# Routing counts and key-list transposes each placed one step later in the TensorE program of a two-layer MoE backbone

## Chip, cores and metric

The kernel runs on one core of one Trainium2 chip. The metric is the device time of one execution in microseconds (us), the median of three runs. One further execution was taken by the hardware profiler; all rows below come from it.

## The reference

Two layers over 256 tokens of width 1024 (128 context tokens, 128 latent tokens). Each layer has a token-mixing part (three kinds of attention, merged and projected) and a mixture-of-experts part. Only the second matters here:

```
scores = sigmoid(x @ router_w);  biased = scores + router_bias
keep the 4 best of 8 groups of 8 experts, then the 6 best experts of a token
gates  = scores of those six, normalised, times 2.5
routed = sum over experts of gate * (silu(x @ w_gate) * (x @ w_up)) @ w_down   # 64 experts, hidden 256
shared = (silu(x @ shared_w_gate) * (x @ shared_w_up)) @ shared_w_down
y      = x + g2 * rms_norm(routed + shared)
```

Everything is float32. The experts' weights are 64 x 3 MB a layer and are used once.

## The kernel before

Every engine has its own program, written out by hand in the order in which it runs; semaphores join them. So an engine that waits holds up all that is written behind the wait, and nothing is reordered. "Layer" below is the Python loop `for l in range(DEPTH)`, with l = 0 first and l = 1 second.

**Weights.** SyncE (SP) loads every weight block into a ring of 12 slots of 1 MB in SBUF: 60 blocks a layer (one slot each), then 96 double blocks for the experts (two slots, 2 MB each). A load is issued when TensorE (PE) has freed its slots (`ring_free`, raised by `release` at a matmul); PE waits for a landing with `arrived` or `arrived_pair`. The next layer's first blocks follow the last experts' loads through the same ring.

**Routing.** PE forms the router's logits; VectorE (DVE) works out which six experts each token takes (`sel`, L1740, raises `sel_ready`), then the gate weights (L1743 to L1747) and the first half of the shared expert's hidden rows (`shared_hidden(0)`, L1699 and L1700). Meanwhile PE computes the shared expert: `shared_gate_up(t)` for token tile t is eight row steps k = 0 to 7, each one matmul of 128x128 by 128x512, which the trace shows as two instructions (float32 takes two passes). After some steps of `shared_gate_up(1)` PE waits for `sel_ready` and does the **routing counts**: column sums of `sel` (L989, L990), ranks of the tokens of experts 0 and 1 (L992 to L994, raises `ranks_done`), and two transposes of `sel` (L510, raises `keys_tr`). Then it finishes the steps.

DVE turns ranks and keys into `first_hot` (four instructions, L1758, `first_hot_ready`), which picks the tokens of the first expert pair; PE multiplies with it in `first_tokens` (L1002, L1005, `first_done`); DVE writes the first gather's row numbers (L1763, `first_rows`), does `shared_hidden(1)`, and enters the experts' loop.

**Key lists.** In that loop DVE extracts for each expert its up to 64 tokens: eight rounds of MAX8 and MATCH_REPLACE8 on `keys` (L1791/L1793 and L1796). The last MAX8 (L1793) raises `list_ready`. PE transposes the lists (`transpose_lists`, L1032, `list_tr`); DVE copies them (L1798) and writes the row numbers of all other pairs (L1799, `rows_ready`), and GpSimd (POOL) starts the indirect gathers of pairs 1, 2, ... (L498).

**Experts' loop.** 32 pairs of experts. For a pair g PE does `gate_up(g)` (L1050): eight row steps k, each two experts e side by side in two column halves, so four instructions a step; two experts together. Then `transpose_hidden(g)` (L510, waits for DVE's L1812), `down(g)` (L1076) and `combine(g)` (L1099). The order at the start is: transposes of pair 0's tokens, `gate_up(0)` with `transpose_lists` inside it, `transpose_inputs(1, 0)` (L510, waits for pair 1's gather), `transpose_hidden(0)`, `transpose_inputs(1, 1)`, `down(0)`, `gate_up(1)`. ScalarE (ACT) copies PSUM to SBUF (L1331) and does the tanh of the gates (L1338), DVE the products (L1804, L1812).

Of the kernel before, what the change touches and what calls it, by code (L numbers as in the profile page):

```python
# [32 lines left out]
KC = D // P  # L33
# [99 lines left out]
def hybrid_layers(nc, a, o):  # L133
    with ExitStack() as ctx:
# [191 lines left out]
        def wide(n):  # L326

            return ring[:, n % RING_SLOTS, :].rearrange("p (k n) -> p k n", k=4)
# [177 lines left out]
        def _(pe):  # L506
# [15 lines left out]
            for l in range(DEPTH):  # L522
# [3 lines left out]
                def arrived(n):  # L526

                    pe.wait_ge(ring_in[n % RING_SLOTS], (l * ROUNDS + n // RING_SLOTS + 1) * 16)

                def arrived_pair(n, base):  # L530

                    count = base + (n // RING_SLOTS + 1)
                    pe.wait_ge(pair_in[n % RING_SLOTS // 2], count * 16)
# [11 lines left out]
                def release(first, loads=1):  # L545
                    first.then_inc(ring_free, loads)
# [77 lines left out]
                for j in range(2):  # L624
# [3 lines left out]
                    for m in range(2):  # L628
                        for i in range(KC):
                            k = i % 2 * 4 + i // 2  # L630
# [305 lines left out]
                def token_rows(t, half):  # L936

                    for c in range(4):
                        last = transpose(PS[:, 4 + 2 * t + half, c * P:(c + 1) * P], h2T[:, 4 * half + c, t * P:(t + 1) * P])
                    last.then_inc(htok_tr, 1)  # L940

                def shared_gate_up(t, steps=range(KC)):
                    for k in steps:
                        if t == 0 and k % 4 == 0:
                            arrived(L_SH + k // 4)
                        last = pe.matmul(PS[:, 2 + t, :], h2T[:, k, t * P:(t + 1) * P], wide(L_SH + k // 4)[:, k % 4, :],  # L946
                                         start=(k == 0), stop=(k == KC - 1))
                        if t == 1 and k == 4:
                            release(last)
                    if k == KC - 1:  # L950
                        last.then_inc(shared_gu, 1)
# [31 lines left out]
                logits(1)  # L983
                for half in range(2):
                    token_rows(1, half)
                shared_gate_up(1, range(5))

                pe.wait_ge(sel_ready, l + 1)
                pe.matmul(PS[:, 0, 0:N_EXPERTS], ones, sel[:, 0, :], start=True, stop=False)  # L989
# [5 lines left out]
                for t in range(2):  # L995
                    last = transpose(PS[0:N_EXPERTS, 1, P + t * P:P + (t + 1) * P], sel[:, t, :])
                last.then_inc(keys_tr, 1)
                shared_gate_up(1, range(5, KC))

                def first_tokens():  # L1000
                    for t in range(2):
# [18 lines left out]
                with pe.Fori(0, npass) as p:  # L1020
# [6 lines left out]
                    def transpose_lists():  # L1027

                        pe.wait_ge(list_ready, q + 1)
                        apart(pe)  # L1030
                        for e in range(2):
                            last = pe.matmul(PS[e * CAP:(e + 1) * CAP, 2, 0:PAIRS], lists, ident[0:N_EXPERTS, e:N_EXPERTS:2],  # L1032
                                             start=True, stop=True)
                        last.then_inc(list_tr, 1)

                    def gate_up(g):

                        if g:
                            pe.wait_ge(xe_ready, done + (2 * g + 2))
                        for k in range(KC):  # L1040
                            if g == 0 and k % 4 == 0:
                                pe.wait_ge(xe_ready, done + (k // 4 + 1))
                            for e in range(2):
                                n = 6 * g + 2 * (k // 4) + e
                                if k % 4 == 0 and e == 0:
                                    arrived_pair(n, base)
                                if g == 0 and k == 2 and e == 0:
                                    transpose_lists()
                                w = ring[:, n % RING_SLOTS, :].rearrange("p (k c) -> p k c", k=4)
                                last = pe.matmul(PS[e * CAP:(e + 1) * CAP, 0, :], xe[:, k, e * CAP:(e + 1) * CAP], w[:, k % 4, :],  # L1050
                                                 start=(k == 0), stop=(k == KC - 1), skip_group_check=True)
                                if e == 0 and (k == 4 or (k == 0 and g >= 1)):
                                    release(last, 2)
                        last.then_inc(gu_done, 1)
# [54 lines left out]
                    for half in range(2):  # L1109
                        transpose_inputs(0, half)  # L1110
                    gate_up(0)
                    transpose_inputs(1, 0)
                    transpose_hidden(0)
                    transpose_inputs(1, 1)
                    down(0)
                    for g in range(1, PAIRS):
                        more = g + 1 < PAIRS
                        if not more:
                            pe.wait_ge(xe_ready, done + (2 * g + 2))
                            pe.wait_ge(first_hot_ready, uses * 4 + 8)  # L1120
                            first_tokens()
                        gate_up(g)
                        if more:
                            transpose_inputs(g + 1, 0, frees=2)
                        combine(g - 1, 0, frees=0 if more else 2)
                        transpose_hidden(g)
                        if more:
                            transpose_inputs(g + 1, 1)
                        combine(g - 1, 1)
                        down(g)  # L1130
# [804 lines left out]
```

## Time and profile before

| | us |
|---|---|
| three runs | 1704.34, 1704.36, 1705.16 (median 1704.36) |
| the profiled execution | 1704.68 |
| its span, first to last instruction | 1702.9 |
| PE busy in it | 1665.1 (98%) |
| DVE busy | 430.7 (25%) |
| ACT busy | 324.8 (19%) |
| POOL busy | 120.0 (7%) |

The mean granted clock of TensorE is 0.997 of its full speed. PE is busy nearly all the time, so the places where it is not, and what it waits for there, are read one by one from the order in time. The experts' loop of the first layer runs from about 371 to 859 us, that of the second from about 1207 to 1692 us; the change touches the stretch of some 20 us ahead of each and its first pair.

### The profile page before, as it was taken

The page shows a single profiled execution, that of the slowest core. Times are in us where ns is not written, and L with a number is a line of the kernel's source. Part 1 is how long each engine was busy: PE and PEld are TensorE (multiplying, and loading weights), DVE is VectorE, ACT ScalarE, POOL GpSimd, SP SyncE. Part 2 cuts the span into 40 slices and gives each one's busy share as a digit, 9 for nine tenths or more (in the row PEclk, how much of TensorE's full clock was granted, in tenths as well). Part 3 has the DMA queues.
Part 4 walks back from the last instruction along what each step waited for, and adds up shares of the span by engine and source line. Part 5 has one row for each costly group of instructions (what it writes and reads, how often), then busy time and mean ns, then how long its engine had stood idle before and what let it go on. Part 6 is the DMA issues. An engine that isn't in the chain of part 4 may idle for free. (4 is left out here: it accounts for less than half of the span.)

```text
span 1702.9 us, 21074 instructions
## 1 busy us (share of the span) xinstructions
PE 1665.1 (98%) x8107; PEld 892.7 (52%) x8107; DVE 430.7 (25%) x1183; ACT 324.8 (19%) x786; POOL 120.0 (7%) x164
## 2 busy tenths in 40 slices
PE   5999999999999999999999999999999999999998
PEld 3778788543333333333368878884433333333332
DVE  1114444361111111111131444543411111111112
ACT  1010341121111111111120113403111111111111
POOL 3001000020000000001020000001100000000000
PEclk9999999999999999999999999999999999999999
DMA  9994233379999999999999732235899999999993
GB/s 388 397 410 164 76 117 118 118 282 419 425 426 424 425 425 426 425 425 424 420 389 422 292 115 99 99 110 207 323 426 425 426 425 425 426 425 424 426 425 159
DMA packets 61100, 561.94 MB, mean 330 GB/s; under 512 B 13020, under 2 KB 13168, under 8 KB 21072
## 3 DMA queue, kind: packets, MB, share of 16 engines
q1 hardware_dynamic: 45504, 529.55, 75.4%
q0 software_dynamic: 15504, 31.09, 5.3%
q8 instruction: 66, 1.08, 0.3%
q14 instruction: 26, 0.21, 0.0%
HBM read 575.95 MB, written 6.88 MB: 342 GB/s over the span
## 5 line engine op out<-in xcount | busy, mean ns | idle before, releaser
L1050 PE MATMUL PS<-ring,region 128*64 128x512 f32 x2048 | 451.0, 592 | 0.7 <-ACT region L1331 0.7
L1050 PEld LDWEIGHTS PS<-ring,region 128*64 128x64 f32 x2048 | 146.4, 137 | 290.4 <-issue 290.3
L617 PE MATMUL PS<-region,ring 128*128 128x256 f32 x1088 | 245.3, 381 | 0.5 <-DMA ring<-in_blocks 0.5
L1099 PE MATMUL PS<-region 128*128 128x512 f32 x512 | 241.0, 594 | 0.0
L1076 PE MATMUL PS<-ring,region 128*64 128x512 f32 x1024 | 233.8, 598 | 0.2
L617 PEld LDWEIGHTS PS<-region,ring 128*128 128x128 f32 x1088 | 203.8, 190 | 34.2 <-issue 6.3
L1804 DVE SCALAR_TENSOR_TENSOR region<-region,PS 128x256 f32<-128x256 f32 x64 | 26.9, 421 | 662.8 <-ACT region L1338 662.8
L510 PEld LDWEIGHTS PS<-const,region 128*128 128x128 f32 (+1 forms) x925 | 106.5, 141 | 115.7 <-issue 67.3
L510 PE MATMUL PS<-const,region 128*128 128x128 f32 (+1 forms) x925 | 137.8, 278 | 15.7 <-DMA region<-in_c 9.6
L1076 PEld LDWEIGHTS PS<-ring,region 128*64 128x64 f32 x1024 | 67.7, 136 | 157.4 <-issue 156.7
L1344 ACT ACTIVATE region<-PS 128x512 f32<-128x512 f32 x128 | 76.4, 597 | 265.9 <-PE PS L1076 265.9
L1099 PEld LDWEIGHTS PS<-region 128*128 128x128 f32 x512 | 87.3, 190 | 65.6 <-issue 64.4
L498 POOL DMA_INDIRECT region<-h_table,region x62 | 61.3, 989 | 817.7 <-DVE region L1812 752.3
L1338 ACT ACTIVATE region<-PS 128x256 f32<-128x256 f32 x64 | 24.5, 384 | 406.0 <-PE PS L1050 406.0
L1331 ACT ACTIVATE region<-PS 128x512 f32<-128x512 f32 x128 | 76.2, 597 | 132.6 <-PE PS L510 132.6
L856 PE MATMUL PS<-region,ring 128*128 128x256 f32 x384 | 84.1, 380 | 0.0
L856 PEld LDWEIGHTS PS<-region,ring 128*128 128x128 f32 x384 | 72.6, 190 | 10.1 <-issue 0.3
L1812 DVE SCALAR_TENSOR_TENSOR region<-PS,region 64x256 f32<-64x256 f32 x128 | 61.9, 484 | 4.4
L904 PE MATMUL PS<-ring,region 128*128 128x512 f32 x128 | 55.6, 592 | 0.0
L560 PE MATMUL PS<-ring,condT 128*32 128x256 f32 x768 | 47.0, 394 | 6.7 <-DMA ring<-in_blocks 5.4
L1820 DVE TENSOR_SCALAR region<-const,region 128x256 f32<-128x256 f32 x64 | 22.6, 353 | 106.6 <-PE PS L1099 106.6
L1236 ACT ACTIVATE region<-PS,negm 128x128 f32<-128x128 f32 (+1 forms) x96 | 39.0, 415 | 34.8 <-issue 20.2
(270 smaller groups left out, 991.2 us busy)
## 6 DMA issues: line engine op xcount, KB each, us to landing
ring<-in_expert_blocks SPq DMA_DIRECT2D x192, 2048.0 KB, 17.1
ring<-in_blocks SPq DMA_DIRECT2D x120, 1024.0 KB, 19.6
region<-post_rows POOLq DMA_DIRECT2D x8, 512.0 KB, 6.2
h_first<-region POOLq DMA_DIRECT2D x4, 512.0 KB, 6.4
h_table<-region POOLq DMA_DIRECT2D x4, 512.0 KB
region<-in_w_kvk POOLq DMA_DIRECT2D x2, 640.0 KB, 18.6
region<-in_mla_w_ukv POOLq DMA_DIRECT2D x2, 512.0 KB, 21.8
region<-in_post_pack POOLq DMA_DIRECT2D x2, 512.0 KB, 25.4
```

The lines of the kernel that those rows point to most:

```text
L498: pool.indirect_dma_start(xg[:, g % XG, :] if g else xg[:, 0, 0:D], None, table if g else first_table, bass.IndirectOffsetOnAxis(ap=row_i[ ...
L510: return pe.transpose(out, in_, ident[0:n, 0:n])
L560: last = pe.matmul(PS[32 * g:32 * g + 32, MOD_BANK[group], half * 256:half * 256 + 256], condT[:, k, :], w[:, k % 2, 256 * g:256 * g + 256 ...
L617: last = pe.matmul(PS[:, j % 2, m * T:(m + 1) * T], w[:, k, m * P:(m + 1) * P], hT[:, k, :], start=(k == 0), stop=(k == KC - 1))
L856: last = pe.matmul(PS[:, b + n // 2, (n % 2) * T:(n % 2 + 1) * T], w[:, k, jj * P:(jj + 1) * P], src[:, k, :], start=(k == 0), stop=(k == 3))
L904: last = pe.matmul(PS[:, 4 + 2 * t + half, :], merged[:, k, t * P:(t + 1) * P], w[:, k % 4, :], start=(k == 0), stop=(k == KC - 1))
L1050: last = pe.matmul(PS[e * CAP:(e + 1) * CAP, 0, :], xe[:, k, e * CAP:(e + 1) * CAP], w[:, k % 4, :], start=(k == 0), stop=(k == KC - 1), s ...
L1076: last = pe.matmul(PS[e * CAP:(e + 1) * CAP, 2 + half, :], hid[:, f, e * CAP:(e + 1) * CAP], w[:, f, half * HALF:(half + 1) * HALF], start ...
L1099: last = pe.matmul(PS[:, 4 + 2 * t + half, :], hot[:, t * P:(t + 1) * P], og[:, half * HALF:(half + 1) * HALF], start=False, stop=True, sk ...
L1331: act.activation(xe[:, 4 * half:4 * half + 4, :].rearrange("p k s -> p (k s)"), bank(3 if g <= 1 and half else 1), ACT.Copy).then_inc(xe_r ...
L1344: act.activation(og[:, half * HALF:(half + 1) * HALF], bank(2 + half), ACT.Copy).then_inc(og_ready, 1)
L1812: ve.scalar_tensor_tensor(out=hid_rows[rows], in0=PS[rows, 0, 2 * P:4 * P], scalar=gate, in1=act_g[rows], op0=ALU.mult, op1=ALU.mult).then ...
```

## The change

Two steps of PE's program move; nothing is added or taken away, on PE or on any other engine.

```diff
-                shared_gate_up(1, range(5))
+                shared_gate_up(1, range(6))
 
                 pe.wait_ge(sel_ready, l + 1)
...
                 last.then_inc(keys_tr, 1)
-                shared_gate_up(1, range(5, KC))
+                shared_gate_up(1, range(6, KC))
...
-                                if g == 0 and k == 2 and e == 0:
+                                if g == 0 and k == 3 and e == 0:
                                     transpose_lists()
```

The first edit on PE, in both layers: one more row step (L946) of the shared gate/up stands ahead of the wait for `sel_ready` and the counts (L989 and on).

```order
 L934 MATMUL PS<-const,region 128x64 [waits parts_ready]
 L510 MATMUL PS<-const,region 128x128 x8
-L946 MATMUL PS<-ring,region 128x512 x5
+L946 MATMUL PS<-ring,region 128x512 x6
 L989 MATMUL PS<-sel,const 128x64 [waits sel_ready]
 L990 MATMUL PS<-sel,const 128x64
```

Six row steps instead of five come before the counts. Behind the counts and the two key transposes, still on PE, ahead of the wait for `shared_hid`:

```order
 L994 MATMUL PS<-sel,const 128x2
 L510 MATMUL PS<-const,sel 64x128 x2
-L946 MATMUL PS<-ring,region 128x512 x3
+L946 MATMUL PS<-ring,region 128x512 x2
 L510 MATMUL PS<-const,region 128x128 [waits shared_hid]
 L510 MATMUL PS<-const,region 128x128
```

Two steps are left there instead of three. The slot that step k = 4 frees is freed ahead of the counts in both kernels.

The second edit on PE, in `gate_up(0)` of each layer (L1050 a matmul of one expert, L1032 the list transposes, which wait for `list_ready`):

```order
 L533 ISA [waits xe_ready]
 L1050 MATMUL PS<-ring,region 64x512 [waits pair_in0]
-L1050 MATMUL PS<-ring,region 64x512 x3
+L1050 MATMUL PS<-ring,region 64x512 x5
 L1032 MATMUL PS<-const,region 64x32 [waits list_ready]
 L1032 MATMUL PS<-const,region 64x32
-L1050 MATMUL PS<-ring,region 64x512 x4
+L1050 MATMUL PS<-ring,region 64x512 x2
 L1042 REGISTER_ALU
```

The wait for `list_ready` now stands behind six matmuls (three row steps) instead of four, and two instead of four come before the wait for the second half of the weights.

## Rows read from the trace of the kernel before

**Rows 1.** The page: busy time of each engine.
```profile
PE 1665.1 (98%) x8107; PEld 892.7 (52%) x8107; DVE 430.7 (25%) x1183; ACT 324.8 (19%) x786; POOL 120.0 (7%) x164
```
**Rows 2.** Order in time, PE, first layer: start, us, line, shape, count, idle before.
```profile
352.18 4.46 PE L946 MATMUL PS<-ring,region 128*128 128x512 f32 x10
357.44 0.43 PE L989 MATMUL PS<-sel,const 128*128 128x64 f32 x2 [0.80 <-DVE sel L1740]
...
358.80 2.74 PE L946 MATMUL PS<-ring,region 128*128 128x512 f32 x6
361.38 0.38 PE L510 MATMUL PS<-const,region 128*128 128x128 f32 x2
361.60 0.51 PE L1002 MATMUL PS<-const,region 128*128 128x2 f32 x4
```
**Rows 3.** Order in time, DVE, first layer, routing and first tokens.
```profile
357.16 0.23 DVE L1740 TENSOR_SCALAR sel<-region 128x128 f32<-128x128 f32 x1
...
359.47 0.15 DVE L1751 TENSOR_SCALAR ranks<-PS 128x4 f32<-128x4 f32 x1
...
360.11 0.98 DVE L1758 TENSOR_SCALAR region<-const,ranks,sel 128x64 f32<-128x64 f32 x4
...
362.58 0.16 DVE L1763 TENSOR_SCALAR region<-PS 128x1 uint32<-128x1 f32 x1 [0.60 <-PE PS L1005]
```
**Rows 4.** Order in time, PE, first layer, the first pair.
```profile
370.96 1.94 PE L1050 MATMUL PS<-ring,region 128*64 128x512 f32 x8 [0.34 <-ACT region L1331]
373.32 0.30 PE L1032 MATMUL PS<-const,region 64*64 64x32 f32 x4 [0.43 <-DVE region L1793]
373.56 5.37 PE L1050 MATMUL PS<-ring,region 128*64 128x512 f32 x24
379.54 0.66 PE L510 MATMUL PS<-const,region 128*128 128x128 f32 x4 [0.61 <-DMA region<-h_table,region]
380.99 0.84 PE L510 MATMUL PS<-const,region 128*128 128x128 f32 x6 [0.79 <-DVE region L1812]
```
**Rows 5.** Order in time, DVE, first layer, end of the key lists.
```profile
372.76 0.42 DVE L1793 MAX8 region<-region 64x8 f32<-64x256 f32 x1
...
373.95 0.19 DVE L1798 COPY region<-PS 128x32 f32<-128x32 f32 x1
```
**Rows 6.** Order in time, PE, second layer, the same places.
```profile
1193.19 0.43 PE L989 MATMUL PS<-sel,const 128*128 128x64 f32 x2 [0.81 <-DVE sel L1740]
...
1206.71 1.94 PE L1050 MATMUL PS<-ring,region 128*64 128x512 f32 x8 [0.34 <-ACT region L1331]
1208.79 0.30 PE L1032 MATMUL PS<-const,region 64*64 64x32 f32 x4
...
1215.25 0.66 PE L510 MATMUL PS<-const,region 128*128 128x128 f32 x4 [0.85 <-DMA region<-h_table,region]
1216.56 0.84 PE L510 MATMUL PS<-const,region 128*128 128x128 f32 x6 [0.65 <-DVE region L1812]
```
**Rows 7.** Order in time, DVE, second layer.
```profile
1208.23 0.42 DVE L1793 MAX8 region<-region 64x8 f32<-64x256 f32 x1
...
1209.42 0.19 DVE L1798 COPY region<-PS 128x32 f32<-128x32 f32 x1
```
**Rows 8.** Order in time, POOL, first layer: pair 1's gather.
```profile
375.22 1.01 POOL L498 DMA_INDIRECT region<-h_table,region  x1 [9.95 <-DVE region L1799]
```
**Rows 9.** DMA issues at 376.5 us: KB, us to landing; the gather is pair 2's.
```profile
ring<-in_expert_blocks SPq DMA_DIRECT2D x1, 2048.0 KB, 8.5
region<-h_table,region POOLq DMA_INDIRECT x1, 8.7
```
**Rows 10.** Stretches: length, busy of PE, PEld, DVE, ACT, POOL, clock, DMA share, GB/s.
```profile
376.50:380.00 3.50, 2.89 (x16) 0.99 (x12) 0.57 (x2) 0.38 (x1) 0.99 (x1) 1.00 0.86 272
380.00:865.00 485.00, 484.07 (x2190) 186.07 (x2188) 76.78 (x183) 92.08 (x172) 31.77 (x35) 1.00 1.01 424
```
**Rows 11.** Order in time, PE, where the second layer begins.
```profile
865.75 1.07 PE L560 MATMUL PS<-ring,condT 128*32 128x256 f32 x16 [0.70 <-DMA ring<-in_blocks]
```

## The prediction

> **What bounds the kernel now.** The page first: PE is busy 1665.1 us of 1702.9, 98%, and beside its own weight loads (PEld) no engine is over 26% [rows 1]. So the time is PE's own work plus its idle pieces, and a change of order alone can win only idle pieces, or make new ones. The order in time of PE, DVE and POOL around the two edits then shows each idle piece and what ended it. The reader is to see four in each layer: PE waits for `sel` ahead of the counts (0.80 and 0.81 us idle) [rows 2, 6]; for the last MAX8 of the key lists (0.43 in the first layer, unmarked in the second) [rows 4, 6]; for pair 1's gather (0.61, 0.85); and for the hidden rows of pair 0, that is ACT's tanh and DVE's L1812 (0.79, 0.65) [rows 4, 6]. Last, the stretches by DMA share: from 380 to 865 us the 16 DMA engines are full (1.01) while PE is busy 484.07 of 485.00 us [rows 10], and 0.70 of the missing 0.93 is one wait for a weight block, where the second layer begins [rows 11]. In the first layer's experts' loop PE and the weight stream run nearly neck and neck.
>
> **First edit, one step more ahead of the counts.** A pass of a row step takes 0.43 us: six from 358.80 to 361.38 [rows 2]. Five steps are ten passes, 352.18 to 356.48; the counts start at 357.44, because `sel` is written at 357.16 + 0.23 = 357.39, 0.05 earlier [rows 2, 3]. (The 0.80 in the row counts from the modelled end of the last matmul; by starts it is 0.96.) A sixth step is 0.86 us and ends at 352.18 + 12 x 0.43 = 357.34. It fits into the wait with 0.1 us left: the counts start where they did. That is the cover of the moved work, and a thin one; were it gone, the counts would be late by what is missing, but DVE reads the ranks only at 359.47 [rows 3], when PE has long been at the next steps, from 358.80 [rows 2]. So up to half a us would be free.
>
> Behind the counts two steps are left, so PE comes to the transposes at 360.52 instead of 361.38, to `first_tokens` (L1002) at 360.74 instead of 361.60. There a new wait appears: `first_hot` is ready at 360.11 + 0.98 = 361.09 [rows 3], with the same 0.05 PE can start at 361.14. Of the 0.86 won, 0.46 stays. Out of an idle engine two short matmuls take 0.43 instead of 0.38 (L989 against L510) [rows 2], so I take 0.1 off: 0.36 us, bounds 0.30 and 0.46. Queued behind this new wait are only PE's own later steps.
>
> Who follows: DVE's L1763 waits for L1005 with 0.60 us idle [rows 3], so it comes 0.36 earlier, and with it everything in DVE's order: `shared_hidden(1)`, the eight rounds, the last MAX8. PE's shared down and pair 0's transposes run in one piece up to `gate_up(0)`, which starts at 370.60 instead of 370.96. SP's load that waits for the last shared down's release is 0.36 earlier too. In the second layer the same differences hold.
>
> **Second edit, the list transposes behind step k = 2.** First layer before: `gate_up(0)` starts at 370.96, steps 0 and 1 end at 370.96 + 4 x 0.43 = 372.68, the transposes start at 373.32: 0.64 idle by starts, since the MAX8 ends at 372.76 + 0.42 = 373.18 [rows 4, 5]. After: steps 0 to 2 end at 370.60 + 2.58 = 373.18; the lists are there at 372.82 plus the same 0.14, 372.96. No wait. The transposes cost 0.24 as before (373.32 to 373.56), then five steps of 0.86: `gate_up(0)` ends at 377.72, where it was 373.56 + 5.16 = 378.72. Gain 1.00 = 0.36 + 0.64. Second layer: the idle time there is 1208.79 - (1206.71 + 1.72) = 0.36 [rows 6], the MAX8 ends at 1208.65 [rows 7], 0.36 earlier in the new kernel, and PE is there at 1208.93: gain 0.36 + 0.36 = 0.72.
>
> The lists now wait for PE, not PE for the lists; is anybody late by that? DVE's copy L1798 comes after its own MATCH_REPLACE8, at 373.95, though PE's transposes end at 373.62 [rows 4, 5]. After: DVE is free for it at 373.59, the transposes end at 373.18 + 0.30 = 373.48: 0.36 earlier. In the second layer they end at 1208.93 + 0.30 = 1209.23, against a copy at 1209.42 [rows 7] that could have come at 1209.06: 0.15 to 0.19 earlier only. Pair 1's gather moves by as much: issued at 374.86 instead of 375.22 [rows 8], usable at 379.18 instead of 379.54; in the second layer at 1215.08 instead of 1215.25 [rows 4, 6]. It is the next wait in PE's order. Its four transposes take 0.44, and behind them PE waits for the hidden rows, which hang on the end of `gate_up(0)` and so come at 380.99 - 1.00 = 379.99 and 1216.56 - 0.72 = 1215.84. The gather's transposes are done at 379.62 and 1215.52. So the whole 1.00 and 0.72 reach `down(0)`, with 0.37 and 0.32 us to spare. Before, these margins were 1.01 and 0.87: they are what pays for the gain.
>
> **What is left of it at the end.** In the second layer nothing comes behind the experts' loop but PE's own work and the outputs, so 0.72 stays if the ring does not run dry. In the first layer PE's gain ends at the wait for a block [rows 11]: PE is there a full us earlier and waits longer, unless the stream is earlier as well. The stream begins with the load freed 0.36 earlier, and goes on with loads freed in `gate_up(0)`, a whole us earlier (the one issued at 376.5 [rows 9]). Between 376.5 and 380 the engines moved at a share of 0.86, later at 1.01 [rows 10]: 0.15 x 3.5 = 0.53 us of unused time, which the earlier loads fill. So the stream shifts by 0.36 + 0.53 = 0.89; its bounds are 0.36 (only its start moves) and 1.00 (every load was release-bound). I take 0.9.
>
> Sum against the profiled execution: 1704.68 - 0.9 - 0.72 = 1703.06. The median of the three runs is 0.32 below that execution, so the forecast is 1702.8, 0.1% under the 1704.36 of before.
>
> **A rule on the queues.** Pair 2's gather, issued at 376.5 while a weight load was starting, took 8.7 us [rows 9]; pair 1's, 1.3 us ahead of that, was usable after 379.54 - 375.22 = 4.3 us [rows 4, 8]. The Trainium skill (DMA: Bandwidth & Descriptors, "Queues, rings and completion order") says that each DMA engine takes turns between its queues, a packet at a time. It speaks against this change: the more weight packets stand in the other queue, the longer a gather takes. The pair of durations agrees in direction; by this rule the gather would be later than in my sum, which puts weight on the rival below.
>
> **Rivals.**
> - Slower: pair 1's gather meets the weight load. The load after it is issued a whole us earlier, the gather only 0.36 (second layer 0.72 and 0.17). So the lead shrinks from 1.3 to 0.7 us. If it takes the loaded duration, 8.7 us, it is usable at 374.86 + 8.7 = 383.56, 4.38 later than in my sum with 0.37 to spare: the first layer loses 4.0 - 1.0 = 3.0, of which the 0.70 at the layer's end can hide a part (2.3 left); the second 4.38 - 0.32 - 0.72 = 3.3. Sum +5.6: 1710.0. It decides from 0.37 us of delay on. Against: between 376.5 and 380 most of the gather's time already ran beside that load [rows 9, 10]. In full 3%. In a small form, a us late, it takes 0.6 and 0.7 of the gains: about 1704.0; 15%.
> - Stream-bound: the weight stream shifts by 0.36 only. Then the first layer gives 0.36: 1703.3. For it: the full DMA engines; against: the 0.86 share. 16%.
> - The edit does nothing because a neighbouring wait takes it all: with `first_hot` an idle start dearer than taken and the ring dry in the second loop, 1704.3. The order of PE shows both steps moved, so this is about time, not about the program. 5%.
> - More than forecast: later waits close as well, 1701.5. 4%.
> - The forecast, 1702.8, 57%; its own range is 1702.3 to 1703.3.
>
> **Numbers.** The range must hold the time 8 times in 10: 1701.8 to 1704.4, which takes in the small gather delay and the stream's bounds. About 0.2% (3.4 us) is what a measurement of this kernel can tell from no change. Only the full gather case lies above that; with something unseen, slower 4%, faster 3%, within 93%.
>
> **What would show it.** Counts still at 5.26 us after the start of the L946 row; a new PE idle of about 0.4 ahead of L1002, released by DVE L1758; no idle ahead of L1032 in either layer; `gate_up(0)` ending 1.0 and 0.7 earlier against the counts; a wait for the gather still there, and one for L1812 behind it; a wait for the block at the second layer's start of about 0.8 instead of 0.70; span 1701.3. I am wrong if the counts start later, if L1032 still waits, or if the gather's usable time after its issue grows beyond 4.7 us.

## The result and the profile after

The changed kernel takes 1718.45 us (median of 1716.91, 1718.13, 1719.13 and 1718.76), against 1704.63 us for the kernel before (four runs, 1704.34 to 1705.16): 1.0076 times as long, with a 95% interval of 1.0064 to 1.0089. The forecast was 1702.8 us in a range of 1701.8 to 1704.4, so the kernel became slower where it was to become faster, and the time lies outside the range. The profiled execution is the lowest of the four, 1716.91 us.

The page of the changed kernel, as in [rows 1], and its line for the short transposes:

```profile
span 1715.1 us, 21074 instructions
PE 1670.5 (97%) x8107; PEld 895.8 (52%) x8107; DVE 431.1 (25%) x1183; ACT 324.8 (19%) x786; POOL 120.3 (7%) x164
L510 PE MATMUL PS<-const,region 128*128 128x128 f32 (+1 forms) x925 | 140.4, 283 | 24.9 <-DMA region<-h_table,region 13.8
```

The span is 12.2 us longer, PE's busy time 5.4 us: some 7 us are new idle time, and 5 are work that took longer. The last row tells where to look: the transposes waited 13.8 us for data that came from `h_table`, a gather. In the kernel before, this line had 15.7 us of waits in all, 9.6 of them for the constants `in_c`, and 0.61 and 0.85 for this gather [rows 4, 6].

PE in order of time, first layer (start, busy us, what, then in brackets the idle time ahead and what ended it); answers to [rows 2, 4]:

```profile
352.01 5.32 PE L946 MATMUL PS<-ring,region 128*128 128x512 f32 x12
357.27 0.43 PE L989 MATMUL PS<-sel,const 128*128 128x64 f32 x2
...
360.98 0.61 PE L1002 MATMUL PS<-const,region 128*128 128x2 f32 x4 [0.25 <-DVE region L1758]
...
370.44 2.79 PE L1050 MATMUL PS<-ring,region 128*64 128x512 f32 x12 [0.34 <-ACT region L1331]
373.17 0.30 PE L1032 MATMUL PS<-const,region 64*64 64x32 f32 x4
373.40 4.51 PE L1050 MATMUL PS<-ring,region 128*64 128x512 f32 x20
384.67 2.40 PE L510 MATMUL PS<-const,region 128*128 128x128 f32 x10 [6.76 <-DMA region<-h_table,region]
387.00 4.01 PE L1076 MATMUL PS<-ring,region 128*64 128x512 f32 x16
390.84 7.03 PE L1050 MATMUL PS<-ring,region 128*64 128x512 f32 x32
```

The same in the second layer, answering to [rows 6]:

```profile
1214.88 4.51 PE L1050 MATMUL PS<-ring,region 128*64 128x512 f32 x20
1226.38 2.40 PE L510 MATMUL PS<-const,region 128*128 128x128 f32 x10 [7.00 <-DMA region<-h_table,region]
1228.71 4.69 PE L1076 MATMUL PS<-ring,region 128*64 128x512 f32 x16
1233.24 2.31 PE L1050 MATMUL PS<-ring,region 128*64 128x512 f32 x10
```

Everything up to the end of `gate_up(0)` is as forecast or nearly so. Then PE stands still for 6.76 and 7.00 us, where it waited 0.61 and 0.85 for the same gather [rows 4, 6]. And ten transposes then take 2.40 us. Who issued what, from POOL's and SP's rows (a start, the time in issue) and the view of DMA issues (KB, us from issue to landing), first layer; answers to [rows 8, 9]:

```profile
374.80 1.01 POOL L498 DMA_INDIRECT region<-h_table,region  x1 [9.69 <-DVE region L1799]
```

```profile
375.52 0.34 SPq L360 DMA_DIRECT2D ring<-in_expert_blocks  x1
```

```profile
ring<-in_expert_blocks SPq DMA_DIRECT2D x1, 2048.0 KB, 9.3
region<-h_table,region POOLq DMA_INDIRECT x1, 9.8
```

The weight load now follows the gather after 0.73 us (before 1.32; second layer 0.76, before 1.35; the times in the rows are rounded, so a difference of two can be off by 0.01), and the gather lands 0.16 us ahead of that whole 2 MB load, at 384.63 against 384.79. Below I call the time from POOL's issue of the gather to SP's issue of the next load the **lead**, and from POOL's issue to the start of PE's transposes the **gather time**.

The windows of the changed kernel (stretch and sum, then busy us of PE, PEld, DVE, ACT and POOL, the granted clock, the DMA share, GB/s):

```profile
378.00:380.00 2.00, 0.00 (x0) 0.00 (x0) 1.39 (x3) 0.34 (x1) 0.00 (x0) 1.00 0.98 407
380.00:382.00 2.00, 0.00 (x0) 0.00 (x0) 0.00 (x0) 0.00 (x0) 0.99 (x1) 0.73 1.00 422
382.00:384.00 2.00, 0.00 (x0) 0.00 (x0) 0.00 (x0) 0.00 (x0) 0.00 (x0) 0.50 0.65 259
384.00:386.00 2.00, 1.33 (x6) 1.33 (x7) 0.00 (x0) 0.18 (x1) 0.00 (x0) 0.50 0.26 98
386.00:388.00 2.00, 2.00 (x9) 1.10 (x10) 0.78 (x2) 1.02 (x2) 0.00 (x0) 0.56 0.65 131
388.00:390.00 2.00, 2.00 (x12) 0.58 (x10) 0.00 (x0) 0.60 (x1) 0.00 (x0) 1.00 0.79 311
```

While PE is idle, from 377.91 on, the granted clock falls to 0.50, that is 1.2 instead of 2.4 GHz, and it stays there while PE is at work again (from 384.67), for some 3 us. In the second layer it lasts longer, 4 to 5 us:

```profile
1228.00:1230.00 2.00, 2.00 (x8) 0.91 (x8) 0.74 (x2) 0.73 (x2) 0.00 (x0) 0.50 0.66 131
1230.00:1232.00 2.00, 2.00 (x10) 0.57 (x8) 0.00 (x0) 0.26 (x1) 0.00 (x0) 0.79 0.86 356
```

That is the work that took longer. In the first layer, from 382 us on, the DMA engines run empty as well: the next load needs slots that only PE's later steps free.

### The profile page after: what moved, and what is told of

It reads as the page before. It is cut to its first block and busy times, and to the rows that moved or that the text cites. A ratio compares the mean times of both kernels' runs of the same rounds, so it can differ in the third digit from the quotient of the medians.

```text
span 1715.1 us, 21074 instructions
## 1 busy us (share of the span) xinstructions
PE 1670.5 (97%) x8107; PEld 895.8 (52%) x8107; DVE 431.1 (25%) x1183; ACT 324.8 (19%) x786; POOL 120.3 (7%) x164
## 5 line engine op out<-in xcount | busy, mean ns | idle before, releaser
L1050 PE MATMUL PS<-ring,region 128*64 128x512 f32 x2048 | 450.9, 592 | 0.7 <-ACT region L1331 0.7
L1050 PEld LDWEIGHTS PS<-ring,region 128*64 128x64 f32 x2048 | 146.3, 137 | 290.5 <-issue 290.4
L510 PE MATMUL PS<-const,region 128*128 128x128 f32 (+1 forms) x925 | 140.4, 283 | 24.9 <-DMA region<-h_table,region 13.8
L856 PEld LDWEIGHTS PS<-region,ring 128*128 128x128 f32 x384 | 72.6, 190 | 10.1 <-issue 0.3
L1812 DVE SCALAR_TENSOR_TENSOR region<-PS,region 64x256 f32<-64x256 f32 x128 | 61.9, 484 | 4.4
```

Of the source, the lines that this page charges most:

```text
L510: return pe.transpose(out, in_, ident[0:n, 0:n])
L856: last = pe.matmul(PS[:, b + n // 2, (n % 2) * T:(n % 2 + 1) * T], w[:, k, jj * P:(jj + 1) * P], src[:, k, :], start=(k == 0), stop=(k == 3))
L1812: ve.scalar_tensor_tensor(out=hid_rows[rows], in0=PS[rows, 0, 2 * P:4 * P], scalar=gate, in1=act_g[rows], op0=ALU.mult, op1=ALU.mult).then ...
```

## Experiments

The theory from the two profiles (A): the load, issued 0.85 us earlier against the routing counts, takes the gather's bandwidth, and the clock adds to it. Rivals: (B) it is PE's own program, with another cause for the long gather, such as the fetch of instructions; (C) the whole loss is the wait, the clock costs nothing; (D) the gather is served only once the load is through. The expectations of e1, e2 and e4 call another rival C: that the first edit makes the gather late.

All gather times and leads, first / second layer, in order of the lead. The leads and gather times are those of the one profiled execution of each kernel. The column "us" is the median of the runs; where there are several, the ratio to the kernel before, timed beside them, follows with its 95% interval (the medians of the kernel before lay between 1704.63 and 1705.04). "One run" is a single time, which can be a us or two off.

| run | lead | gather time | us | ratio |
|---|---|---|---|---|
| e4_before_release_k3 | 0.47 / 0.51 | 9.3 / 10.2 | 1717.27 | 1.0069 [1.0053, 1.0084] |
| the changed kernel | 0.73 / 0.76 | 9.9 / 10.1 | 1718.45 | 1.0076 [1.0064, 1.0089] |
| e2_lists_only | 0.73 / 0.77 | 9.8 / 9.8 | 1719.22 | 1.0078 [1.0062, 1.0093] |
| e5_fill_idle | 0.73 / 0.76 | 9.8 / 9.8 | 1713.65 | 1.005 [1.0033, 1.0067] |
| e7_load_later_4 | 0.73 / 0.76 | 10.1 / 10.0 | 1716.72 | one run |
| e8_load_later_8 | 0.73 / 0.77 | 10.0 / 9.8 | 1718.21 | one run |
| e6_half_gather | 0.73 / 0.77 | 5.7 / 3.8 | 1704.02 | one run |
| e14_six_list | 1.09 / 1.11 | 4.6 / 5.1 | 1704.32 | one run |
| e13_one_small | 1.15 / 1.17 | 4.2 / 4.8 | 1704.64 | one run |
| before | 1.32 / 1.35 | 4.3 / 4.6 | 1704.63 | 1 |
| e11_light_stream | 1.32 / 1.35 | 4.3 / 5.4 | 1704.35 | 0.9995 [0.9985, 1.0004] |
| e1_counts_only | 1.32 / 1.35 | 4.5 / 5.2 | 1704.64 | 0.9997 [0.9988, 1.0006] |
| e9_three_small | 1.36 / 1.39 | 4.3 / 5.0 | 1704.46 | one run |
| e3_both_release_k5 | 1.59 / 1.62 | 4.6 / 4.9 | 1704.94 | 1.0002 [0.9993, 1.0011] |
| e12_light_stream_both_k5 | 1.59 / 1.62 | 4.4 / 5.0 | 1703.29 | 0.9992 [0.9983, 1.0001] |
| e10_mixed_layers | 1.32 / 2.48 | 4.5 / 5.1 | 1705.36 | 0.9999 [0.999, 1.0008] |

**Which edit.** e1 has the first edit alone (`range(6)`; the lists stay at `k == 2`), e2 the second alone (`range(5)`, `k == 3`).

> Only the first edit (counts behind six steps); the list transposes stay behind step k = 1. In the changed kernel pair 1's gather is issued at 374.80 and the next weight load at 375.52, a lead of 0.72 us, and the gather takes 9.83 us; before, the lead was 1.32 us and it took 4.3. Theory A (the lead decides): PE still waits for the last MAX8, so gather and load both come 0.4 to 0.5 earlier, the lead stays 1.3, the gather takes about 4.3 us, and each layer gains about 0.45: 1703.8. Rival C (the first edit, by moving DVE and POOL earlier against something else, is what makes the gather late): some 14 us slower, near 1718.

> Only the second edit (list transposes behind step k = 2). Theory A: step k = 4, and with it the load, comes about 0.6 us earlier in the first layer and 0.4 in the second, while the gather, whose row numbers wait for DVE or for PE's transposes, does not come earlier; the lead falls to about 0.7 us, the gather takes 9 to 10 us and PE waits some 7 us for it in each layer: about 1718. Rival C (the first edit is to blame): 1704 or a little less.

The first alone changes nothing that can be measured in the time (1704.64 us, a ratio of 0.9997; 1703.8 was expected); the second alone costs all of the loss. So the first edit is not to blame. PE in e2, and the gather's wait in e1:

```profile
384.77 2.40 PE L510 MATMUL PS<-const,region 128*128 128x128 f32 x10 [6.67 <-DMA region<-h_table,region]
```

```profile
379.11 0.66 PE L510 MATMUL PS<-const,region 128*128 128x128 f32 x4 [0.82 <-DMA region<-h_table,region]
```

**Load or program.** e3 keeps both edits and frees the slots for that load one step later in pair 0. e4 takes the kernel before, with neither edit, and frees them earlier.

```diff
e3, against the changed kernel
-  if e == 0 and (k == 4 or (k == 0 and g >= 1)):
+  if e == 0 and (k == 4 + 1 * (g == 0) or (k == 0 and g >= 1)):
       release(last, 2)
e4, against the kernel before
-  if e == 0 and (k == 4 or (k == 0 and g >= 1)):
+  if (g == 0 and k == 3 and e == 1) or (g and e == 0 and k in (0, 4)):
       release(last, 2)
```

> Both edits, and in the first pair alone the two slots of the first half of gate/up are freed at step k = 5 instead of k = 4, so that the next load is issued 0.86 us later; all else as in the changed kernel. Theory A: lead 0.72 + 0.86 = 1.58 us, the gather takes 4 to 4.5 us, PE's wait for it is under 1 us, and the second layer keeps about 0.8 us, the first what its weight stream allows (0 to 0.4): 1703.2 to 1703.9. Rival B (a 16 KB instruction fetch, which in the changed kernel falls on 376.5 us, inside the gather, and before on 385, holds the gather up): the load's issue changes nothing, 1717 to 1719.

> The kernel before, with both edits absent; only in the first pair the two slots are freed by the last matmul of step k = 3 instead of the first expert's of k = 4, so that the load is issued some 0.2 to 0.4 us earlier and the lead is about 0.9 to 1.1 us. Theory A: the gather gets slower though no instruction of PE moved; between the two known points (1.32: 4.3 us; 0.72: 9.8 us) I expect 5 to 9 us for the gather and a time of 1706 to 1717. Rivals B and C: 1704.5, as before.

SP's load and PE's wait in e3, then in e4:

```profile
376.42 0.34 SPq L360 DMA_DIRECT2D ring<-in_expert_blocks  x1
```

```profile
379.39 1.48 PE L510 MATMUL PS<-const,region 128*128 128x128 f32 x10 [1.43 <-DMA region<-h_table,region]
```

```profile
375.98 0.34 SPq L360 DMA_DIRECT2D ring<-in_expert_blocks  x1
```

```profile
384.81 2.40 PE L510 MATMUL PS<-const,region 128*128 128x128 f32 x10 [5.60 <-DMA region<-h_table,region]
```

The changed program with a late load has no loss; the old program with an early load has nearly the whole. That load came earlier than I had meant (a lead of 0.47 instead of 0.9 to 1.1), so e4 says nothing on the leads between. That the load's issue, and not PE's order or its instruction fetch, makes the gather long is shown from both sides. The fetch falls inside the gather in e3 too (16 KB at 376.8 us), and the gather takes 4.6 us. B falls.

What the load does to the gather is seen in the view of DMA queues, cut to the stretch from 1.5 to 3.7 us after the gather's issue (packets, MB, share; q0 carries the gathers, q1 the loads). The kernel before, then the changed kernel:

```profile
q1 hardware_dynamic: 34, 0.34, 56.9%
q0 software_dynamic: 142, 0.21, 37.5%
```

```profile
q1 hardware_dynamic: 34, 0.44, 56.8%
q0 software_dynamic: 37, 0.07, 28.9%
```

And e4 in the first 4.0 us after the gather's issue, in which no packet of q0 is seen (in the second layer 102 of q1, none of q0):

```profile
q1 hardware_dynamic: 95, 1.29, 95.5%
```

From its issue to PE's transposes the gather of the kernel before moves 144 packets, so 142 in this stretch is nearly all of it. At 0.73 us of lead a quarter of them move in the same stretch, and at 0.47 the gather has not even begun.

**The clock.** e5 is the changed kernel with PE kept busy in the wait. The matmuls write a bank that nobody reads.

```diff
                     gate_up(0)
+                    for _ in range(7):
+                        pe.matmul(PS[:, 3, :], ident, const[:, 0:512], ...)
                     transpose_inputs(1, 0)
```

> The changed kernel, and between gate/up of the first pair and the transposes of pair 1's tokens PE does seven more matmuls of 128x128 by 128x512 (7 x 0.86 = 6.0 us) on constants into a PSUM bank that is free there. They fill most of the 7 us in which PE waits for the late gather. In the changed kernel the granted clock falls to 0.50 at the end of that wait and is back only after some 6 us; by rows before and after, the work from the gather's landing to gate/up of pair 1 takes 6.2 and 6.9 us instead of 4.9. Theory A with the clock as a second cost: the gather is as late as before, but the clock stays at 1.00, so 3 to 5 us of the 14 come back: 1713 to 1715. If the clock is no cost of its own: 1718.

PE in e5, then the windows of e5, and of the changed kernel over the same stretches:

```profile
377.98 6.28 PE L1113 MATMUL PS<-const 128*128 128x512 f32 x14
384.73 1.31 PE L510 MATMUL PS<-const,region 128*128 128x128 f32 x10 [0.47 <-DMA region<-h_table,region]
```

```profile
378.00:384.00 6.00, 6.00 (x16) 2.56 (x14) 1.39 (x3) 0.38 (x1) 0.99 (x1) 1.00 0.87 358
384.00:390.00 6.00, 5.45 (x29) 2.42 (x30) 0.78 (x2) 1.97 (x4) 0.00 (x0) 1.00 0.65 211
```

```profile
378.00:384.00 6.00, 0.00 (x0) 0.00 (x0) 1.39 (x3) 0.34 (x1) 0.99 (x1) 0.74 0.88 362
384.00:390.00 6.00, 5.33 (x24) 3.02 (x26) 0.78 (x2) 1.79 (x3) 0.00 (x0) 0.69 0.57 180
```

The gather is as late as before, but the clock stays at 1.00 and ten transposes take 1.31 us instead of 2.40. By medians 1718.45 - 1713.65 = 4.8 us of the 13.8 are the clock's, and 8.7 are left against the kernel before (1713.65 - 1704.94; each pair was timed with its own runs of the kernel before, hence the 0.3 that is missing in the sum). Every run of e5 is faster than every run of the changed kernel. C falls. In the profiled executions the way from the gather to `gate_up(1)` is 1.3 us shorter in the first layer (6.17 against 4.87) and 2.0 in the second (6.86 against 4.88), 3.3 in all.

That the medians give 1.5 us more fits the profiles: the profiled execution of the changed kernel is the fastest of its four, 1.5 us below their median, and how long the clock stays low differs from one execution to the next. In e2, profiled at 1719.15 us, it is still at 0.50 when in the changed kernel it was back at 1.00:

```profile
388.00:390.00 2.00, 2.00 (x8) 0.71 (x6) 0.00 (x0) 0.00 (x0) 0.00 (x0) 0.50 0.75 287
390.00:392.00 2.00, 2.00 (x10) 0.57 (x8) 0.00 (x0) 0.60 (x1) 0.00 (x0) 0.82 1.09 467
```

The same two ways take 7.60 and 7.59 us there, 5.4 more than in e5; in e8 (1718.21 us) they take 6.90 and 7.56, 4.7 more.

**What holds the gather up.** e6 is the changed kernel with pair 1's gather cut to 64 of its 128 rows; it leaves out the tokens of pair 1's second expert.

> The changed kernel, but pair 1's gather fetches the rows of its first expert only, 64 of 128 partitions; the tokens of its second expert are left out. Theory A in its finer form (each of the 16 DMA engines takes turns between a packet of the weight load and one of the gather, 8 of each, so gather and load end together, 384.63 and 384.79 us): with 4 turns instead of 8 the gather ends about half way through the load, some 6 to 7.5 us after its issue instead of 9.8. Rival D (the gather simply stands behind the load and is served when that is done): it still lands with the load, 9.5 us or more after issue.

PE in e6, and its gather in the view of DMA issues:

```profile
380.74 1.31 PE L510 MATMUL PS<-const,region 128*128 128x128 f32 x10 [2.54 <-DMA region<-h_table,region]
```

```profile
region<-h_table,region POOLq DMA_INDIRECT x1, 5.6
```

With the lead unchanged at 0.73, half the rows come after 5.7 and 3.8 us, while the load needs 8.3 and 8.5. So the gather isn't kept back until the load is through, and D falls. Its own amount of data counts, as it would if the two queues took turns; but both times are below the 6 to 7.5 us that I had worked out from even turns, so that working doesn't hold in numbers. By the rule named in the prediction (Trainium skill, DMA: Bandwidth & Descriptors, "Queues, rings and completion order") they take turns packet by packet. The changed kernel's 34 packets beside 37 in the stretch above agree with it in kind, and so does e6; e4's 95 beside none is more than turns explain, and why the gather begins so late there is open.

**Where the edge is.** I tried to set the load later in small steps. e7 and e8 put four and eight empty instructions on SP between its wait and the load; e9 and e13 put three and one transposes of a constant on PE ahead of step k = 4, which frees the slots; e14 puts six more 64x64 by 64x32 matmuls behind the list transposes.

```diff
e7 (e8: 8 instead of 4)
+                    for _ in range(4 * (n == 0)):
+                        sp.nop()
                     sp.dma_start(ring[:, slot:slot + 2, :] ...
e9 (e13: without the loop, one)
+                                if g == 0 and k == 4 and e == 0:
+                                    for _ in range(3):
+                                        transpose(PS[:, 3, 0:P], const[:, P:2 * P])
e14
                         last.then_inc(list_tr, 1)
+                        for i in range(6):
+                            pe.matmul(PS[..., 1, 0:PAIRS], lists, ident[...], ...)
```

> The changed kernel with four empty instructions on SP between its wait for the freed slots and the issue of the weight load that meets the gather; I guess 0.2 to 0.3 us, so a lead of about 1.0 us between the known 0.72 (9.8 us) and 1.3 (4.3 us). If the gather's time falls evenly with the lead: about 7 us and a span of some 1708. If there is an edge: either about 4.5 us (span 1703) or about 9.5 (span 1715).

> As the run with four, with eight empty instructions: a lead of 1.1 to 1.3 us. Evenly: 5 to 6 us. With an edge somewhere below 1.3 us: 4.3 to 4.6 us for the gather and a span of 1702 to 1703.

> The changed kernel, with three more small transposes (0.11 us each) on PE between steps k = 3 and k = 4 of the first pair's gate/up, into a PSUM bank that is free there: step k = 4 and the weight load come 0.33 us later, the gather does not move. The empty instructions on SP had left the lead at 0.73 and 0.77 us, so this is the first point between: about 1.05 us. If the gather's time falls evenly from 9.8 us at 0.72 to 4.3 at 1.32: about 7 us, span near 1708. With an edge: 4.5 us (span 1702.5 to 1703) or 9.5 us (span 1715).

> As the run with three more small transposes between steps k = 3 and k = 4, with one. Three moved the load by 0.64 us against the gather (lead 1.36), more than their 0.33, since PE also changes from half to full columns and back; one should move it by 0.64 - 0.22 = 0.42: lead 1.14 us. Even fall between 0.77 (10.0 us) and 1.31 (4.5 us): 6.2 us. Edge: 4.3 to 5 or 9.5 to 10 us.

> The changed kernel with six more matmuls of the form of the list transposes (64x64 by 64x32) right behind them, into a bank that is free there, without a change of columns: 0.2 to 0.4 us, lead 0.9 to 1.1 us. Even fall: 6.5 to 8.5 us for the gather. Edge: 4.3 to 5 or 9.5 to 10 us.

e7 and e8 missed: the lead stayed at 0.73, so they say nothing on the edge. e9 moved it by 0.64, twice what I had counted on, which brought it back to that of the kernel before; e13 and e14 came out at 1.15 and 1.09. PE in e13, then in e14:

```profile
379.48 0.66 PE L510 MATMUL PS<-const,region 128*128 128x128 f32 x4 [0.61 <-DMA region<-h_table,region]
```

```profile
379.53 0.66 PE L510 MATMUL PS<-const,region 128*128 128x128 f32 x4 [1.13 <-DMA region<-h_table,region]
```

The table then reads as an edge. At leads from 0.47 to 0.77 us the whole gather takes 9.3 to 10.2, at 1.09 to 2.48 it takes 4.2 to 5.4; between 0.77 and 1.09 nothing was measured. So a third of a us of lead is worth some 5 us of gather. One number lies in that gap: POOL is busy for 1.01 us with the instruction that issues the gather [rows 8], so at the short leads the load is issued before that ends, at the long ones after it. Whether that is what makes the edge was not tested.

**Where the first layer's gain went.** In e3 the gather is early, and PE is 0.84 us ahead at `gate_up(1)` (counts to `gate_up(1)`: 27.12 us, before 27.96), yet its time is that of the kernel before. In the second layer it is 0.51 ahead at the same place (27.27 against 27.78), which is about the 0.4 us by which its profiled span is shorter, and less than the medians can tell. PE in e3 where the second layer begins, answering to [rows 11]:

```profile
865.43 1.07 PE L560 MATMUL PS<-ring,condT 128*32 128x256 f32 x16 [1.35 <-DMA ring<-in_blocks]
...
888.62 1.56 PE L647 MATMUL PS<-region,ring 128*128 128x256 f32 x6 [0.74 <-DMA ring<-in_blocks]
```

The two waits were 0.70 and 0.21 before, and together are 1.18 longer: the gain is waited away. From the first layer's counts to the second's it is 835.75 us before and 835.99 in e3. To see whether it is the stream, e11 is the kernel before with a lighter stream, and e12 the same with both edits and the late release. Both load 1 MB instead of 2 where the down blocks of a pair's second expert are due in the even pairs, and leave that expert's down weights out.

```diff
+                    if n == 4:
+                        sp.dma_start(ring[:, slot, :], ... part, :, 0:2048 ...)
+                        return
```

> The kernel before, with one weight load in six of the experts' loop fetching 1 MB instead of 2 (the down weights of the second expert of each even pair are left out, what lies in the slot is used). The stream is then no longer neck and neck with PE. The waits for a block at the second layer's start (0.70 and 0.21 us) go: about 0.9 us below the kernel before, 1704.0. It is the base for the run beside it.

> Both edits with the release at k = 5, and the same light stream (down weights of the second expert of each even pair left out). Theory: in the full kernel the first layer's 0.97 us (gate/up of pair 1 at 384.43 against 385.40) was taken by the weight stream. Without that limit it stays: 0.9 + 0.5 = 1.4 us below the run with the light stream alone. Rival: it is lost elsewhere, and the difference is 0.4 as between the same two kernels with the full stream.

e11 takes 1704.35 us, e12 1703.29. In neither does PE wait for a block at the transition. PE's counts in e12, both layers:

```profile
357.57 0.43 PE L992 MATMUL PS<-sel,const 128*128 128x64 f32 x2
1192.20 0.43 PE L992 MATMUL PS<-sel,const 128*128 128x64 f32 x2
```

That is 834.63 us between them, and 835.49 in e11: now 0.86 of the first layer's gain arrives. With 0.40 from the second layer (27.38 against 27.78) that is the 1.3 us by which e12's profiled span is shorter than e11's (expected 1.4). The medians differ by 1.06 us, in the same direction but within what two such medians can tell. Of the 0.9 us that e11 itself was to win, its counts show only 0.26 (835.49 against 835.75): with the wait for the block gone, PE waits 0.81 us for DVE behind it.

**A version for use.** e10 has the first edit in both layers, the second in the second layer only, with that load's release two steps later there.

```diff
-                                if g == 0 and k == 3 and e == 0:
+                                if g == 0 and k == 2 + l and e == 0:
                                     transpose_lists()
...
-                                if e == 0 and (k == 4 or (k == 0 and g >= 1)):
+                                if e == 0 and (k == 4 + 2 * l * (g == 0) or (k == 0 and g >= 1)):
```

> The first edit in both layers; the second edit in the second layer alone, and there the two slots are freed at step k = 6 instead of 4, a lead of about 2.4 us. Theory A, with the weight stream taking the first layer's gain (so that the load must come as early there as the gather allows): first layer 0 to 0.1 us, second layer 0.7 to 0.9: 0.8 below the kernel before, about 0.5 below both edits with k = 5. That is near what the runs can tell; the profile's stretches should show it.

It takes 1705.36 us against 1705.01: nothing won. Its gather took 5.1 us at a lead of 2.48, half a us more than before, and the clock was at 0.50 for some 3 us behind the wait for it (1.93 us) in its profiled execution, the slowest of eleven. e3 and e12 waited 1.75 and 1.87 us at the same place without that, so the wait alone doesn't bring it about. No run here beats the kernel before by more than the measurement can tell.

## Why the prediction was wrong, step by step

- **What bounds the loop: a reading was wrong.** "0.70 of the missing 0.93 is one wait for a weight block": that wait lies before 865.75 [rows 11], outside the stretch from 380 to 865. What is missing inside it is mostly the 0.79 us for L1812 at 380.99 [rows 4]. So PE waits for no block inside the loop; the block is short only where the next layer begins.
- **First edit: right.** The counts start 5.26 us after the L946 row, as before. The new wait ahead of L1002 is 0.25 us, released by L1758 (forecast 0.4), and `gate_up(0)` starts 0.35 earlier against the counts (forecast 0.36).
- **Second edit on PE: right in kind.** No idle time ahead of L1032 in either layer. The six passes take 2.73 us (370.44 to 373.17) where I had 2.58, so `gate_up(0)` ends 0.85 and 0.56 earlier against the counts, not 1.00 and 0.72.
- **The gather's issue: smaller than forecast.** It comes 0.25 us earlier in the first layer (forecast 0.36), and not at all in the second (forecast 0.17): DVE's copy L1798 now waits for PE's transposes, which the forecast put to exactly that moment.
- **The step that failed** is "usable at 379.18 instead of 379.54; in the second layer at 1215.08". It moved the gather with its issue and held its duration at 4.3 us. The duration hangs on the load behind it. The load came 0.85 us earlier, the lead sank from 1.32 to 0.73, and the gather took 9.9 and 10.1 us. e3 and e4, which move nothing but the load's issue, take the loss away and bring it about.
- **The rival "pair 1's gather meets the weight load" is what happened.** Its lead of 0.7, its point of decision and its direction were right. Its price in the sum, 5.6 for both layers, was too low and its chance, 3%, far too low. In the first layer it had 3.0, less 0.7 for the wait at the layer's end; the profile has 5.6 with hardly any relief: a gather of 9.9 instead of 8.7 us (+1.2), the clock (+1.3), and a wait at the end that fell only from 0.70 to 0.53. The load after that one was late too, issued at 386.17 instead of 381.46. In the second layer 3.3 became 6.7: +1.4 for the gather, +2.0 for the clock. The sum of 12.3 is the profile's 12.2. The clock stood in no term of the sum or of a rival.
- **Why I gave it 3%.** "Between 376.5 and 380 most of the gather's time already ran beside that load" counted time, as if the engines' share were what mattered. But in the kernel before the gather was 1.3 us old when the load came. I had one gather at 1.3 us of lead and 4.3 us, one issued together with a load and 8.7 us [rows 9] (and that one stood behind pair 1's in the same queue, so it was no clean price either), and no row between; the honest bounds of the new duration were 4.3 and 8.7, and a lead of 0.7 is nearer to the crowded one. Both ends belonged into the range; the measured 9.9 and 10.1 are above even the upper one.
- **The stream: not borne out, and hidden by the rest.** "0.53 us of unused time, which the earlier loads fill" made 0.9 us of the first layer. In e1 the load is issued 0.35 us earlier against the counts and `gate_up(1)` starts 0.34 earlier, but the second layer's counts come only 0.04 earlier (835.71 against 835.75), less than the lower bound of 0.36. In e14 the load is 0.50 earlier and 0.08 arrives. These are single profiled executions. e3 lost all of its 0.84, but its load is issued as late as before (19.11 us after the counts, before 19.10); it shows that a PE that is ahead inside the loop gains nothing when the stream is not, and e12 shows the gain kept with a lighter stream. A load 0.85 us earlier together with a short gather was not run.

## What to carry to other kernels

When an edit moves a step that frees a buffer, work out what transfer it starts and which short transfer that one will overtake or crowd: the distance between two issues is a quantity of its own, and a margin in it can end in an edge. If the trace has a short transfer's duration once nearly alone and once crowded, and the change moves it between these, both belong into the range with real weight. Place the release of the next load so that the load is issued well behind the short gather; in this kernel one row step later was enough (e3). And where TensorE must wait several us for one thing, count the clock of the work behind it too.

## What the runs showed of the hardware that I had not expected

- The gather of 128 rows took 4.2 to 5.4 us at a lead of 1.09 us or more, and 9.3 to 10.2 at 0.77 or less; 64 rows at leads of 0.73 and 0.77 took 5.7 and 3.8.
- At a lead of 0.47 no packet of the gather moved in the first 4.0 us after its issue, while the load's queue moved 95 (e4).
- In the two waits of 6.76 and 7.00 us without a matmul the granted clock fell from 1.00 to 0.50, and it stayed there while PE worked again, for some 3 us in the first layer and 4 to 5 in the second, and for 5 to 6 in both layers of e2 (there by windows of 1 us). By the profiled executions two such waits cost 3.3 (the changed kernel) to 5.4 us (e2) beside the waits themselves. Matmuls of no use in the wait kept it at 1.00 (e5).
- Four or eight empty instructions ahead of SP's load moved its issue by less than 0.05 us against the gather's (e7, e8).

What stays open: why at the shortest lead the gather's packets begin so late, where between 0.77 and 1.09 us the edge lies and what sets it, and what makes the clock stay low longer in one execution than in another.
